# Expert weights in two half transfers per buffer, with a used signal for each half

## What is computed

```python
def grouped_moe(x, router_w, router_b, w_gate, w_up, w_down):
    ...
    for e in range(N_EXPERTS):          # 16, D_EXPERT = 512
        h = jax.nn.silu(t @ w_gate[e]) * (t @ w_up[e])
        y = y + combine[:, e:e + 1] * (h @ w_down[e])
```

## Time and profile before

| | us |
|---|---|
| median of 3 runs | 1612.54 (1612.41 to 1612.89) |
| the profiled execution | 1612.92 |
| its span, first to last instruction | 1611.1 |
| PE busy | 1539.3 (96%) |
| VectorE, ScalarE busy | 699.5, 453.7 |
| mean rate of the 16 DMA engines | 327 GB/s |

### The profile page before, as it was taken

One profiled execution on the slowest core, in us unless ns is written; L12 is line 12 of the kernel. 1 busy time (PEld: TensorE's weight loads), 2 busy tenths in 40 slices (PEclk: granted clock), 3 DMA queues, 4 the chain that ended last, 5 costly groups with the idle time before them and its releaser, 6 DMA issues.

```text
span 1611.1 us, 18456 instructions
## 1 busy us (share of the span) xinstructions
PE 1539.3 (96%) x7630; PEld 901.1 (56%) x7630; DVE 699.5 (43%) x1010; ACT 453.7 (28%) x600; POOL 9.5 (1%) x19
## 2 busy tenths in 40 slices
PE   9999999999999989899889999999999999999994
PEld 7888787885343343343338888887434335344332
DVE  5545567635333332332247474463544233233325
ACT  5334466424020111011036363252411102111102
POOL 0010000000000000000000000000000000000000
PEclk9999999999999999999999999999999999999998
DMA  8665234577999999999997555456799999999996
GB/s 325 250 196 205 105 131 159 189 295 281 399 427 427 428 426 429 428 427 428 424 412 300 184 200 185 158 204 274 286 428 429 427 428 427 427 427 428 428 422 244
DMA packets 50886, 527.47 MB, mean 327 GB/s; under 512 B 5579, under 2 KB 5643, under 8 KB 12530
## 3 DMA queue, kind: packets, MB, share of 16 engines
q1 hardware_dynamic: 49586, 522.27, 79.3%
q0 software_dynamic: 1216, 4.02, 0.8%
HBM read 524.17 MB, written 2.10 MB: 327 GB/s over the span
## 4 chain that ended last, share of the span: by engine, by line
PE 73%; DMA 21%; DVE 2%; SPq 1%; ACT 1%; issue 0%; DVEq 0%; ACTq 0%
PE bank L1344 25%; DMA w_all<-in_moe_w_down 17%; PE bank L850 10%; PE bank L852 10%; PE bank L851 10%; PE bank L1302 4%; DMA w_all<-in_moe_w_gate_up 3%; PE bank L1412 2%; SPq L749 1%; PE bank L1502 1%; DMA w_land<-in_ev_w_in 1%; PE bank L1315 1%; PE bank L1427 1%; PE bank L862 1%; PE bank L1395 1%; PE bank L914 1%
## 5 line engine op out<-in xcount | busy, mean ns | idle before, releaser
L1344 PE MATMUL bank<-w_all,xg 128*64 128x512 f32 x2016 | 450.8, 596 | 18.6 <-DMA w_all<-in_moe_w_gate_up 17.1
L1344 PEld LDWEIGHTS bank<-w_all,xg 128*64 128x64 f32 x2016 | 138.7, 137 | 296.2 <-issue 259.1
L850 PE MATMUL bank<-w_hi,T_hi 128*128 128x512 f32 x736 | 290.4, 395 | 2.9 <-DVE w_lo L2242 1.5
L852 PE MATMUL bank<-w_hi,T_lo 128*128 128x512 f32 x736 | 286.8, 390 | 0.0
L851 PE MATMUL bank<-w_lo,T_hi 128*128 128x512 f32 x736 | 286.5, 389 | 0.0
L2166 DVE TENSOR_TENSOR w_lo<-w_land,w_hi 128x2048 fp32r<-128x2048 f32 x90 | 205.0, 2290 | 177.5 <-ACT w_hi L1702 177.3
L1702 ACT CAST w_hi<-w_land 128x2048 fp32r<-128x2048 f32 x94 | 178.1, 1910 | 217.7 <-PE bank L852 215.6
L2727 DVE TENSOR_TENSOR y_lo<-bank,y_hi 128x512 fp32r<-128x512 f32 x54 | 37.3, 692 | 425.1 <-ACT y_hi L1965 425.1
L2738 DVE SCALAR_TENSOR_TENSOR X<-bank,weight,X 128x512 f32<-128x512 f32 x224 | 152.4, 743 | 50.1 <-PE bank L1412 50.1
L850 PEld LDWEIGHTS bank<-w_hi,T_hi 128*128 128x128 f32 x736 | 138.2, 188 | 35.2 <-issue 4.3
L852 PEld LDWEIGHTS bank<-w_hi,T_lo 128*128 128x128 f32 x736 | 138.2, 188 | 29.1
(11 more groups left out here) (368 smaller groups left out, 1345.3 us busy)
## 6 DMA issues: line engine op xcount, KB each, us to landing
w_all<-in_moe_w_gate_up SPq DMA_DIRECT2D x124, 2048.0 KB, 21.1
w_all<-in_moe_w_down SPq DMA_DIRECT2D x56, 2048.0 KB, 23.2
w_land<-in_od_w_in SPq DMA_DIRECT2D x32, 1024.0 KB, 4.9
w_land<-in_ev_w_in SPq DMA_DIRECT2D x31, 1024.0 KB, 5.0
w_land<-in_ev_w_out SPq DMA_DIRECT2D x16, 1024.0 KB, 4.9
w_land<-in_od_w_out SPq DMA_DIRECT2D x16, 1024.0 KB, 4.8
w_all<-in_moe_w_down SPq DMA_DIRECT2D x12, 1024.0 KB, 28.0
w_land<-in_att_w SPq DMA_DIRECT2D x7, 1024.0 KB, 4.8
```

The source lines that it names most:

```text
L850: pe.matmul(dst, hi_l, hi_r, start=start, stop=False)
L852: return pe.matmul(dst, lo_l, hi_r, start=False, stop=stop)
L1344: ins = pe.matmul(dst[halves[h], :], cols(c), U.weights(q, pos + h)[:, c, :], start=start and c == 0, stop=stop and c == 3)
```

## The change

Pairs 8 to 90 of each layer (83 pairs) are transferred as two halves of 1 MB. The first half has the rows `c` = 0 and 1 of both units, the second the rows 2 and 3. The first lands on a new semaphore of the buffer, `half_in`, the second on `pair_in`. PE waits for the first half ahead of `c` = 0 and for the second ahead of `c` = 2, and adds 1 to `used` behind `c` = 1 and 1 behind `c` = 3, where it added 2 at the end. SP waits for the first of these signals before it issues a first half, and for the second before a second half. Where the buffer was last used by the wide expert, SP waits for the whole pair in both cases, and `down_wide` waits for both halves ahead of its first matmul.

```diff
+        half_in = [sem(f"half_in{p}") for p in range(len(RING_PAIRS))]
...
+            def halves(self, n):
+                return n != EARLY_PAIR and n >= 8 and n < N_PAIRS - 5
...
-            def freed(self, n):
+            def freed(self, n, half=1):
...
-                    return 4 * self.sb0 + 2 * before + 2
+                    wide = self.layer and 6 * WIDE <= before + 2 < 6 * WIDE + 12
+                    return 4 * self.sb0 + 2 * before + (2 if wide else 1 + half)
...
+                        if U.halves(n):
+                            src = moe_src(layer, number[at_e] if layer and at_e >= 4 else at_e, part, j)
+                            for k, done in ((0, half_in[p]), (1, pair_in[p])):
+                                sp.wait_ge(used, U.freed(n, k))
+                                sp.dma_start(two_rows(w_all[:, 2 * p:2 * p + 2, :], 2 * k), two_rows(src, 2 * k)) \
+                                    .then_inc(done, 16)
+                            return
...
+                        elif two:
+                            pe.wait_ge(*U.half_landed(q, pos))
                         else:
                             pe.wait_ge(*U.landed(q, pos))
                         for c in range(4):
-                            if in_halves and c == 2:
+                            if (in_halves or two) and c == 2:
                                 pe.wait_ge(*U.landed(q, pos))
...
-                        if not again:
-                            ins.then_inc(used, 2)
+                            if c % 2 and not again:
+                                ins.then_inc(used, 1)
...
+                        pe.wait_ge(*U.half_landed(q, pos))
                         pe.wait_ge(*U.landed(q, pos))
                         unit(0, 0)
...
+                        pe.wait_ge(*U.half_landed(q, pos + 2))
                         pe.wait_ge(*U.landed(q, pos + 2))
```

More of the change, by code:

```diff
@@ L601, in landed, with half_landed @@
                 return pair_in[p], 16 * (self.layer * len(pairs_in(p)) + turn_of(n)[0] + 1)
-            def freed(self, n):
+            def halves(self, n):
+                return n != EARLY_PAIR and n >= 8 and n < N_PAIRS - 5
+            def half_landed(self, q, pos):
+                n = self.number(q, pos)
+                p = pair_of(n)
+                mine = [k for k in pairs_in(p) if self.halves(k)]
+                return half_in[p], 16 * (self.layer * len(mine) + mine.index(n) + 1)
+            def freed(self, n, half=1):
                 p = pair_of(n)
@@ L1335, in two_units @@
                         in_halves = last and pos == 42
+                        two = U.halves(U.number(q, pos))
                         if in_halves:
                             pe.wait_ge(gate_half_in, 16 * (layer + 1))
+                        elif two:
+                            pe.wait_ge(*U.half_landed(q, pos))
                         else:
```

## The result

The changed kernel takes 1651.92 us (median of 4 runs, 1650.36 to 1653.82) against 1612.47 for the kernel before beside it: a ratio of 1.0247 with a 95% interval of 1.0235 to 1.0259. The forecast was 1654, the range 1636 to 1670.

The account below looks back on a forecast made before the run. The prediction took the saturated DMA weight stream to bound the experts' stages. Per layer, 22.4 us lost to slower 4 KB stretches less 1.8 gained at the start gave 41.2 us for both: 1654 us, range 1636 to 1670.

Parts of the forecast that it names:

- What bounds the kernel: Experts' stages: the saturated DMA weight stream sets their end, 4.90 us a pair, while PE needs only 4.34.
- Part 2: Steady expert stream: 4 KB stretches lower 428 to 405 GB/s, 0.28 us more a pair, 22.4 us a layer.
- the scaling of the short windows to a DMA share of 1.004: Layer-end windows' rates, brought to the steady stream's share, gave 405, 405 and 401 GB/s; 405 was taken.
- three rows (399, 391, 399): Layer-end windows already moving 4 KB stretches: 399, 391 and 399 GB/s at shares 0.99, 0.97 and 1.00.
- The best of the earlier trace: Layer-end window at 410 GB/s, taken as the optimistic bound: 5.115 us a pair, 0.215 more.
- The figure of the Trainium skill: For the expert stream: 408.7 GB/s with 4 KiB rows, so 5.13 us a pair and an estimated 33 us in all.
- The rival by the same page's rule on bandwidth: Expert stream keeps its rate, 4.90 us a pair; only the earlier start counts, 1604 to 1609 us; chance 6%.
- Part 1: Start of each layer's expert stream: two-step release sends pair 11 sooner, gaining 1.8 us a layer, bounds 0 to 4.2.
- the sum: Both experts' stages: 22.4 lost less 1.8 gained is 20.6 us a layer, 41.2 for both.
- Part 3: SP's extra issues and holds, PE's extra waits and signals in the experts' stages: costed at nothing.
- Marks named ahead: Expected profile signs: 600 to 700 us at about 405 GB/s, share 1.00 or above, four times the packets.
- The round of 36.3 us in the chain: Expert stage's chain of waits: a buffer's round of seven pairs should take 36.3 us in place of 34.3.

Follow-up runs that it names:

- e4: Against the kernel before: whole-pair transfers kept, only PE's signal per pair split in two, with SP waiting for both; 1612.46 us, ratio 1.0004.
- e9: Against e3: each pair's two 1 MB transfers cut into even and odd partitions, 16 KB stretches; 1613.50 us, ratio 1.0009.
- e1: Against the changed kernel: same half transfers with 4 KB stretches, but PE waits for both halves and signals once per pair; 1653.75 us, ratio 1.0269.
- e2: Against e1: the two 1 MB transfers cut between the pair's two units, giving 8 KB stretches; 1625.51 us, ratio 1.0089.
- e7: Against the changed kernel: halves only for pair 11 of each layer, all other pairs land whole; 1616.06 us, ratio 1.0030.
- e6: Against the changed kernel: halves only for pairs 8 to 11 of each layer, all other pairs land whole; 1615.99 us, ratio 1.0034.
- e3: Against e1: the two 1 MB transfers cut at partition 64, into partitions 0 to 63 and 64 to 127, 16 KB stretches; 2382.74 us, ratio 1.4766.
- e8: The changed kernel measured again, unaltered, beside the other runs on one chip; 1649.59 us, ratio 1.0241 against the kernel before.

## Why the prediction held, point by point

**What bounds the kernel: right.** The stream at its limit sets the end of each experts' stage. Moving its rate from 428 to 421, 409 and 386 GB/s moved the time by 14, 43 and 92 us, and e4 and e9, which left the rate alone, by 1.4 and 1.2.

**Part 2, the rate: right in cause, too large in size.** The step that was mis-sized is the scaling of the short windows to a DMA share of 1.004. That is the steady share of 16 KB packets; in a steady stream of 4 KB packets the weights' queue shows 1.023. Brought to that, three rows (399, 391, 399) would have given 412, 412 and 408 in place of 405, 405 and 401; measured were 409, and 0.23 us a pair in place of 0.28. For 80 pairs: 18.2 us a layer in place of 22.4. The best of the earlier trace rows, 410 GB/s at a share of 1.02, was distrusted because of that share and was the nearest. The figure of the Trainium skill, 408.7 GB/s (DMA: Bandwidth & Descriptors, section on the iDMA fabric), agrees with the measured 409 to 0.1%. The rival by the same page's rule on bandwidth (128 partitions, 1 MiB a transfer) fell: e1 and e2 keep the rule and lose 2.7% and 0.9%, while e9, whose transfers of 1 MiB reach 64 partitions each, does not keep it and loses 0.1%.

**Part 1, the start: wrong.** Forecast was a gain of 1.8 us a layer. The layers grew by 18.95 and 20.35 us, of which the rate explains 18.2: the rest is a loss of 0.75 and 2.15. The step that failed is that an issue 1.8 us sooner means a stream 1.8 us sooner: the sum let a half start like a whole pair. The head start held for the issue (e7), but the halves begin slower than whole pairs do on a queue that has run dry: the window 410 to 420 us moves 379 GB/s at a share of 1.00, where the earlier trace rows have 433.

e1 shows the halves without the head start. Its first issue:

```profile
385.42 4.65 SPq L713 DMA_DIRECT2D w_all<-in_moe_w_down  x4
```

That is 385.42 - 381.80 = 3.62 us behind its first expert matmul. The kernel before issues its pair 3.63 behind (386.93 - 383.30), and e2 its first transfer with 8 KB stretches 3.62 behind (385.20 - 381.58). The first 10 us behind that matmul, of the kernel before, e1, the changed kernel and e2:

```profile
383.30:393.30 10.00, 10.00 (x58) 5.19 (x58) 5.75 (x11) 1.97 (x5) 0.00 (x0) 1.00 0.55 202
```

```profile
381.80:391.80 10.00, 10.00 (x57) 5.19 (x58) 5.69 (x11) 3.04 (x7) 0.00 (x0) 1.00 0.45 118
```

```profile
383.50:393.50 10.00, 10.00 (x58) 5.20 (x58) 5.14 (x10) 1.68 (x4) 0.00 (x0) 1.00 0.64 201
```

```profile
381.60:391.60 10.00, 10.00 (x57) 5.19 (x58) 5.74 (x11) 1.84 (x4) 0.00 (x0) 1.00 0.54 204
```

e1 has moved 84 GB/s x 10 us = 840 KB less than the kernel before, 2.0 us of the stream. The changed kernel's earlier issue makes up for that and no more. e2, two transfers a pair as well, loses nothing, so the slow start goes with the halves of 4 KB stretches and not with having two transfers; why they start slower is not shown. The whole stages agree. e1's chain:

```profile
381.80 7.02 PE bank L1367 x32
...
818.96 24.06 DMA w_all<-in_moe_w_down
...
1160.61 7.02 PE bank L1367 x32
...
1595.07 20.93 DMA w_all<-in_moe_w_down
```

Its layers take 461.22 and 455.39 us, 20.57 and 20.53 more than before: 2.3 to 2.4 us a layer beyond the rate, a cost that the sum did not have. Against these, the changed kernel's two-step release and early first half gave back 1.6 and 0.2 us (one execution each) where 1.8 was forecast.

By the windows under e6 and e7 the changed kernel has moved 10640 KB in layer 0's first 35 us, 0.7 us less than the kernel before; by the forecast it should have been 1.3 us ahead (1.8 sooner, less pairs 11 and 12 at 0.23, since 8 to 10 were to fit in ahead of the gap). The same 35 us in layer 1, before and now:

```profile
1141.40:1176.40 35.00, 34.69 (x173) 14.03 (x174) 13.92 (x29) 7.47 (x15) 0.00 (x0) 1.00 0.81 313
```

```profile
1162.20:1197.20 35.00, 34.69 (x173) 14.05 (x174) 13.82 (x29) 6.11 (x12) 0.00 (x0) 1.00 0.86 289
```

Here it is 24 GB/s x 35 us = 840 KB, 2.0 us behind. So 2.0 us of layer 0's miss of 2.55 and 3.3 of layer 1's 3.95 lie at the starts; the other 0.6 or so of each was not traced. In the sum the two misses, 4.2 us too much and about 3 too little a layer, nearly cancel: 20.6 forecast, 19.6 measured. That the forecast of 1654 came closer than its working is luck.

**Part 3, the rest at nothing: right.** PE's signals (e4) and two transfers in place of one (e9) cost nothing that can be told. SP is held in its issues all through the stage, as was thought possible, and the engines' queue stayed full: share 1.03.

**Marks named ahead.** The window's rate (409 for about 405), the four-fold packets and the share above 1.00 came. The round of 36.3 us in the chain did not, since SP's holds cut the chain into steps of four pairs; per pair they show 5.12 us. SP's first issue came 1.7 us sooner against the first expert matmul (385.41 behind 383.50, before 386.93 behind 383.30), for 1.8. Layer 0's last landing came 19.2 us later (843.10), for some 20.

## What to carry to other kernels

Where a stage runs at the DMA engines' limit, look at the contiguous stretch each descriptor moves before cutting a transfer: in this kernel 16, 8, 4 and 2 KB gave 428, 421, 409 and 386 GB/s, while two transfers of 1 MB in place of one of 2 MB cost nothing that could be told, as long as each spread over all the partitions' range (e9, not e3). Releasing a buffer earlier is worth only what the queue was idle, which is read from the DMA share window by window; in a saturated stretch it is worth nothing (409 GB/s with it and without, the changed kernel and e1). And price a restart after an idle gap from rows of a start with the same stretches, not by the steady rate: here the start of the 4 KB halves took back what the earlier issue gave.

## What was not expected of the hardware

- **Half of the partitions, half of the rate.** Transfers that keep to partitions 0 to 63 or 64 to 127 ran at 215 GB/s with all 16 engines busy (e3); the same bytes by even and odd partitions at 427 (e9).
- **Slow starts.** After an idle gap the stream moves little for some 4 us although the engines are busy for 56% to 75% of that time. From the kernel before, just behind the first issue, and from the changed one:

```profile
386.00:390.00 4.00, 4.00 (x22) 1.15 (x17) 2.22 (x4) 0.00 (x0) 0.00 (x0) 1.00 0.56 156
```

```profile
386.20:390.20 4.00, 4.00 (x22) 1.15 (x17) 1.62 (x3) 0.00 (x0) 0.00 (x0) 1.00 0.75 164
```

  The halves were issued 1.7 us sooner, the engines are busy 75% of these 4 us in place of 56%, and 5% more has moved.
- **PE's clock at the start of the experts.** In the 7 us around layer 1's first gather the mean granted clock was 0.76 in the changed kernel, so PE ran part of them at the lower of its two levels (1.2 GHz); the kernel before had 1.00 (2.4 GHz). In both PE had stood idle for 1.0 us just before the gather, so that alone doesn't tell them apart. 32 matmuls of the gather took 5.58 us in place of 4.24. First the changed kernel, then the one before:

```profile
1156.00:1163.00 7.00, 6.30 (x36) 5.72 (x38) 4.68 (x11) 6.96 (x13) 0.00 (x0) 0.76 0.31 131
```

```profile
1136.00:1142.00 6.00, 4.97 (x38) 4.37 (x40) 4.61 (x12) 6.00 (x12) 0.00 (x0) 1.00 0.47 199
```

  Such stretches at the lower level came in other places in other runs; in e8's profile this gather took 4.23 us in both layers. This one is 1.3 us of the 40.8 here. Such stretches are likely part of why single runs differ by 2 or 3 us: of the kernel before's runs beside the experiments, the six with a mean clock of 0.996 took 1609.55 to 1610.30 us, the six with 0.992 took 1612.04 to 1612.96.
